# Turning three of four feed-forward tiles with VectorE blocks and partition copies instead of TensorE

## The chip, the cores and the metric

The kernel runs on one core of one Trainium2 chip. Everything is float32. The metric is the device time of one execution in microseconds, as the median of several runs. Shorter is better.

## The reference

Two blocks of a transformer run one after the other over 256 tokens of width 2048. The first block has two layers; each ends in the feed-forward part that the change touches:

```python
D_MODEL = 2048; SEQ = 256; D_FF = 4 * D_MODEL; DEPTH = 2

def squared_relu_mlp(h, w1, w2):
    z = jax.nn.relu(h @ w1)
    return (z * z) @ w2

for i in range(DEPTH):
    ...                                   # pooling or differential attention, memory attention
    x = x + jnp.concatenate([token_out, mem_out], axis=-1) @ w_out[i]
    x = x + squared_relu_mlp(rms_norm(x, ffn_norm[i]), w_ff1[i], w_ff2[i])
```

The second block (a linear recurrence, windowed attention, gates and projections) is not touched.

## The kernel before

**Weights.** All large products are cut into groups of 512 output columns over a contraction of 2048. A group has eight slabs (S = 8) of 256 rows by 512 columns of weight, 512 KB each. SP loads a slab into `raw` (line 740), ScalarE rounds it to `whi` (`hi`, line 876), VectorE computes the rest `wlo = raw - whi` (`lo`, line 1180), and TensorE multiplies: for each of two weight tiles and two token blocks, three matmuls of 512 columns (lines 1683 to 1685), 12 in a slab. There are four slots (RAW = 4): SP may refill a slot once VectorE has read it, and ScalarE may overwrite `whi` once TensorE has multiplied that slot's previous slab. So ScalarE and VectorE run at most some three slabs ahead of TensorE. Groups alternate between two accumulators `acc`.

**Order.** Each engine runs its own program, written slab by slab: first its work on the slab, then the steps that the schedule places behind it. Engines run in order; a step that waits holds everything behind it on that engine.

**Feed-forward.** The 8192 hidden columns are done in four chunks (NCHUNK = 4) of 2048. A chunk has four groups of the first product (w_ff1) and four of the second (w_ff2), 16 groups' worth of x-updates over the layer. Three chunks run as a hardware loop (`Fori`) of eight groups, k = 0 to 7, shifted by one: the loop's k = 0 to 2 are w_ff1 groups 1 to 3, k = 3 to 6 the w_ff2 groups, k = 7 the first w_ff1 group of the next chunk. The last chunk is written out. Behind slab 1 of k = 0 to 3 comes the end of the w_ff1 group that has just been finished: ScalarE takes it out of `acc` with a scale and a ReLU (`epi_relu2`, line 927), VectorE squares it into `stage_b` (line 1212), which holds 256 tokens as two blocks of 128 partitions by 512 columns.

**The tail.** The second product needs the hidden tile with its columns on partitions. Behind slab 3 of the same group, TensorE transposes `stage_b` into the PSUM bank `tp` with eight 128x128 transposes (`tail`, line 1701). Behind slab 5 ScalarE rounds `tp` into `set_hi` (line 992) and VectorE writes the rest into `set_lo` (line 1275). There are four tails in a chunk, 32 in the two layers. In k = 3, TensorE waits ahead of slab 0 for the first three tails and ahead of slab 6 for the fourth.

**x-updates.** Behind slab 1 of k = 4 to 7 VectorE adds a finished w_ff2 group to `x` (line 1650).

**Pool queue.** GpSimd only issues DMAs: `pool_w`, `mem_again` (memory tiles for the second layer), and spills and loads of the second block.

Of the kernel before, what the change touches and what calls it, by code (L numbers as in the profile page):

```python
# [10 lines left out]
TOK = 256  # L11
TB = TOK // P
D = 2048
NK = D // P
GW = 512
# [86 lines left out]
class Schedule:  # L102


    def __init__(self):
        self.groups = []
        self.woven = {}
        self.ends = {}
        self.lent = {}
        self.steps = {e: {} for e in ("pe", "act", "dve", "pool")}  # L110
        self.tails = 0
        self.staged = 0
        self.halves = 0
        self.info = {}
        self.norms = 0
        self.loops = {}
# [96 lines left out]
def plan():  # L213
# [64 lines left out]
    def ffn(layer, rst, a, z, next_rst, next_gain):  # L278

        first = sc.group(f"w_ff1{layer}", 0, 0, a)  # L280
        sc.groups[first].need[0] = [("tail_lo", sc.tails - 1)]
        sc.groups[first].need[S - 2] = [("tail_lo", sc.tails)]
        sc.loops[first + 1] = dict(layer=layer, tail0=sc.tails, staged0=sc.staged, rst=rst, a=a, z=z)
        for _ in range(8 * (NCHUNK - 1)):
            sc.group(None, 0, 0, a)
        sc.tails += 4 * (NCHUNK - 1)
        sc.staged += 4 * (NCHUNK - 1)
# [168 lines left out]
def build(nc, A, out):  # L456
# [6 lines left out]
    with ctx:  # L463
# [92 lines left out]
        def tail_bank(lent):  # L556

            if lent == "sd":
                return sd
            return tp if lent is None else acc[lent % 2]  # L560
# [6 lines left out]
        def pair_scales(i, hh):  # L567
# [12 lines left out]
        out_of = [sem("group_out0"), sem("group_out1")]  # L580
        names = ("tail_tp", "tail_hi", "tail_lo", "staged", "x_stat", "rstd_ok", "stage_th",
                 "att_in", "att_qk", "att_score", "att_smx", "att_exp", "att_prob", "att_pt", "att_ptc",
# [190 lines left out]
        def _(pool):  # L773
# [70 lines left out]
            def x_back(a):  # L844
# [4 lines left out]

            steps = dict(pool_w=pool_w, mem_again=mem_again, x_spill=x_spill, gate_store=gate_store,  # L850
                         gate_load=gate_load, merge_store=merge_store, merge_load=merge_load, lru_w=lru_w,
                         x_back=x_back)
            for s in sorted(sc.steps["pool"]):
                for name, args in sc.steps["pool"][s]:
                    steps[name](*args)


        @block.scalar
        def _(act):
# [122 lines left out]
            def tail(t, dst, kt, gain, lent=None):  # L982
                t = t if isinstance(t, N) else N(t)
                tp = tail_bank(lent)
                act.wait_ge(sm["tail_tp"], at(t + 1))
                if dst == "ut":
                    ins = A_(ut_tiles(kt, 2), tp[:, 0:2 * TOK].rearrange("p (n t) -> p n t", n=2), ACT.Copy)
                elif dst == "gt":
                    act.wait_ge(sm["x_out"], 16)
                    ins = A_(gt[:, TOK * kt:TOK * (kt + 2)], tp[:, 0:2 * TOK], ACT.Copy)  # L990
                elif gain is None:
                    ins = A_(sets[dst][0][:, TOK * kt:TOK * (kt + 4)], tp[:], ACT.Copy)  # L992
# [147 lines left out]
            for kind, g, info in segments():  # L1140
# [4 lines left out]
                else:  # L1145
                    with act.Fori(0, NCHUNK - 1) as c:
                        cc = N(0, 1, c)
                        for k in range(8):
                            for s in range(S):
                                hi(cc * 8 + (g + k), s)  # L1150
                                q = cc * 4 + (info["staged0"] + k)
                                t = cc * 4 + (info["tail0"] + k)
                                if s == 1 and k < 4:
# [7 lines left out]
        def _(dve):  # L1161
# [98 lines left out]
            def tail(t, dst, kt, gain, lent=None):  # L1260
# [11 lines left out]
                h, l = sets[dst]  # L1272
                if gain is None:
                    c = slice(TOK * kt, TOK * (kt + 4))
# [7 lines left out]
                ins.then_inc(sm["tail_lo"], 1)  # L1282


            def per_head(t, like, width):
# [315 lines left out]
            def epi_last(g, i):  # L1601
# [5 lines left out]
                for b in range(TB):  # L1607
# [6 lines left out]
                         epi_sigm=epi_sigm, epi_proj_a=epi_proj_a, epi_proj_b=epi_proj_b, x_rstd=x_rstd,  # L1614
                         tail=tail, norm_sum=norm_sum, norm_root=norm_root, norm_scale=norm_scale,
                         norm_rope=norm_rope, rope_gains=rope_gains,
# [13 lines left out]
            for kind, g, info in segments():  # L1630
# [4 lines left out]
                else:  # L1635
                    with dve.Fori(0, NCHUNK - 1) as c:
                        cc = N(0, 1, c)
                        for k in range(8):
                            for s in range(S):
                                lo(cc * 8 + (g + k), s)  # L1640
                                q = cc * 4 + (info["staged0"] + k)
                                t = cc * 4 + (info["tail0"] + k)
                                if s == 1 and k < 4:
                                    epi_relu2(cc * 8 + (g + k - 1), info["rst"], q, t)
                                if s == 5 and k < 4:
                                    tail(t, info["z"], 4 * k, None)
# [17 lines left out]
        def _(pe):  # L1664
# [215 lines left out]
            for kind, g, info in segments():  # L1880
# [7 lines left out]
                else:  # L1888
                    with pe.Fori(0, NCHUNK - 1) as c:
                        cc = N(0, 1, c)  # L1890
                        for k, (w, r, col, src) in enumerate(loop_groups(info, cc)):
                            for s in range(S):
                                if k == 3 and s in (0, S - 2):
                                    pe.wait_ge(sm["tail_lo"], at(cc * 4 + (info["tail0"] + (3 if s == 0 else 4))))
# [76 lines left out]
```

## Time and profile before

| | us |
|---|---|
| median of 3 runs | 3082.58 (3082.22 to 3083.31) |
| profiled execution, its own time | 3082.89 |
| its span in the trace | 3081.1 |
| TensorE matmul busy | 3024.2 |
| VectorE busy | 1760.4 |
| ScalarE busy | 1498.4 |
| GpSimd busy | 51.0 |

The granted TensorE clock is 0.997 of full speed over the span. The profiled execution is 1.8 us longer than its span and 0.3 us above the median of the runs. Times in the trace are microseconds from the span's start.

### The profile page before, as it was taken

Reading aid. Unit: us, or ns where it says so; the run is one execution under the profiler, and the core shown is the slowest. Engines: PE = TensorE matmul, PEld = TensorE weight load, DVE = VectorE, ACT = ScalarE, POOL = GpSimd, SP = SyncE. Lnnn points to the kernel's source line nnn. Section 1 sums busy time; section 2 is a strip of 40 time slices with the busy share of each in tenths; the row PEclk is TensorE's granted clock in tenths of the full one; section 3 lists DMA queues with packets and bytes.
Section 4 is the critical chain, followed back from the end, with each engine's and each line's share of the span. In section 5 each row is a group of like instructions: output and inputs, shape, how many; then the busy total and the mean of one; then the engine's idle time right before and its main releaser. Section 6 shows DMA issues by size and latency. Waiting matters only on the chain.

```text
span 3081.1 us, 37226 instructions
## 1 busy us (share of the span) xinstructions
PE 3024.2 (98%) x13900; PEld 2503.5 (81%) x13900; DVE 1760.4 (57%) x2334; ACT 1498.4 (49%) x2019; POOL 51.0 (2%) x81
## 2 busy tenths in 40 slices
PE   8999999999999999999999999999999999999998
PEld 6877888888888778778888888888888888787886
DVE  6536554545455676865554545455556557786554
ACT  6534434434344565654434444344444547786333
POOL 0000000000000000000000000000000000010000
PEclk9999999999999999999999999999999999999999
DMA  7545565565655555545565665655775555665664
GB/s 255 183 129 173 191 198 184 191 190 187 194 178 185 170 165 158 165 147 188 191 196 186 192 185 190 189 175 199 217 206 180 154 174 166 197 209 198 225 239 151
DMA packets 301161, 573.80 MB, mean 186 GB/s; under 512 B 18640, under 2 KB 43600, under 8 KB 300240
## 3 DMA queue, kind: packets, MB, share of 16 engines
q1 hardware_dynamic: 293248, 541.13, 55.8%
q0 software_dynamic: 7184, 29.63, 2.8%
q8 instruction: 103, 1.69, 0.2%
q10 hardware_dynamic: 576, 0.94, 0.1%
q14 instruction: 50, 0.41, 0.0%
HBM read 561.15 MB, written 10.49 MB: 186 GB/s over the span
## 4 chain that ended last, share of the span: by engine, by line
PE 85%; DVE 7%; ACT 5%; issue 2%; DMA 1%; DVEq 0%; ACTq 0%
PE acc L1683 26%; PE acc L1685 26%; PE acc L1684 26%; PE tp L1701 2%; DVE wlo L1180 2%; ACT whi L876 1%; DVE wlo L1175 1%; PE sd L1764 1%; PE sd L1746 1%; ACT prob L1093 1%; PE sd L1852 1%; ACT qk L1101 0%; ACT whi L879 0%; ACT L1093 0%; DVE set_lo L1279 0%
## 5 line engine op out<-in xcount | busy, mean ns | idle before, releaser
L1683 PE MATMUL acc<-whi,set_hi 128*128 128x512 f32 x4096 | 1620.2, 396 | 25.0 <-DVE wlo L1180 15.8
L1685 PE MATMUL acc<-whi,set_lo 128*128 128x512 f32 x4096 | 1597.3, 390 | 0.0
L1684 PE MATMUL acc<-wlo,set_hi 128*128 128x512 f32 x4096 | 1596.7, 390 | 0.0
L1180 DVE TENSOR_TENSOR wlo<-raw,whi 128x1024 fp32r<-128x1024 f32 x944 | 1130.4, 1222 | 592.6 <-ACT whi L876 591.7
L876 ACT ACTIVATE whi<-raw 128x1024 fp32r<-128x1024 f32 x944 | 969.9, 1057 | 642.1 <-PE acc L1685 611.7
L1683 PEld LDWEIGHTS acc<-whi,set_hi 128*128 128x128 f32 x4096 | 770.4, 188 | 197.7 <-DVE wlo L1180 25.8
L1685 PEld LDWEIGHTS acc<-whi,set_lo 128*128 128x128 f32 x4096 | 770.1, 188 | 162.8
L1684 PEld LDWEIGHTS acc<-wlo,set_hi 128*128 128x128 f32 x4096 | 770.8, 188 | 154.2
L1275 DVE TENSOR_TENSOR set_lo<-tp,set_hi 128x1024 fp32r<-128x1024 f32 x40 | 49.0, 1225 | 197.3 <-ACT set_hi L992 197.3
L992 ACT ACTIVATE set_hi<-tp 128x1024 fp32r<-128x1024 f32 x40 | 41.1, 1026 | 209.4 <-PE tp L1701 209.4
L1175 DVE SCALAR_TENSOR_TENSOR wlo<-raw,par,whi 128x512 fp32r<-128x512 f32 x160 | 111.9, 748 | 53.0 <-ACT whi L879 52.2
L1212 DVE TENSOR_TENSOR stage_b<-stage_a 128x1024 f32<-128x1024 f32 x32 | 39.2, 1225 | 142.2 <-ACT stage_a L927 142.2
L879 ACT ACTIVATE whi<-raw,par 128x512 fp32r<-128x512 f32 x160 | 103.8, 716 | 18.5 <-DMA raw<-in_w_kv 8.1
L927 ACT ACTIVATE stage_a<-acc,small 128x512 f32<-128x512 f32 x64 | 40.6, 686 | 140.3 <-PE acc L1685 140.3
L1279 DVE SCALAR_TENSOR_TENSOR set_lo<-tp,par,set_hi 128x256 fp32r<-128x256 f32 x96 | 39.8, 478 | 72.6 <-ACT set_hi L995 72.6
L995 ACT ACTIVATE set_hi<-tp,par 128x256 fp32r<-128x256 f32 x96 | 37.7, 478 | 71.8 <-PE tp L1701 71.8
L1650 DVE TENSOR_TENSOR x<-acc,x 128x1024 f32<-128x1024 f32 x24 | 29.4, 1225 | 74.9 <-PE acc L1685 74.9
L966 ACT ACTIVATE qk<-x 128x512 f32<-128x512 f32 x40 | 25.0, 632 | 90.5 <-DVE x L1207 90.5
L1701 PEld LDWEIGHTS tp<-const,stage_b 128*128 128x128 f32 x352 | 41.1, 140 | 5.8
L1701 PE MATMUL tp<-const,stage_b 128*128 128x128 f32 x352 | 45.6, 272 | 0.0
L1207 DVE TENSOR_TENSOR x<-acc,x 128x1024 f32<-128x1024 f32 x16 | 19.6, 1224 | 43.3 <-PE acc L1685 43.3
L1069 ACT ACTIVATE set_hi<-sd 128x512 fp32r<-128x512 f32 x12 | 7.2, 598 | 48.1 <-PE sd L1825 48.1
(229 smaller groups left out, 1167.0 us busy)
## 6 DMA issues: line engine op xcount, KB each, us to landing
raw<-in_w_ff SPq DMA_DIRECT2D x512, 512.0 KB, 4.5
raw<-in_w_in SPq DMA_DIRECT2D x248, 512.0 KB, 4.3
raw<-in_w_out SPq DMA_DIRECT2D x96, 512.0 KB, 4.4
raw<-in_w_mem_kv SPq DMA_DIRECT2D x32, 512.0 KB, 4.7
raw<-in_w_proj_a SPq DMA_DIRECT2D x32, 512.0 KB, 4.2
raw<-in_w_proj_b SPq DMA_DIRECT2D x32, 512.0 KB, 5.4
raw<-in_w_kv SPq DMA_DIRECT2D x48, 256.0 KB, 3.3
raw<-in_w_in SPq DMA_DIRECT2D x48, 256.0 KB, 3.7
```

Source lines behind the costliest of these rows:

```text
L876: A_(whi[:, c], raw[:, c], ACT.Copy).then_inc(w_hi, 1)
L879: ins = A_(whi[:, c], raw[:, c], ACT.Copy, scale=gain_of(fold, SLAB_K * s + t))
L927: ins = A_(stage_a[:, GW * b:GW * (b + 1)], a[:, GW * b:GW * (b + 1)], ACT.Relu, scale=rstd[k][:, b:b + 1])
L992: ins = A_(sets[dst][0][:, TOK * kt:TOK * (kt + 4)], tp[:], ACT.Copy)
L1175: ins = V.scalar_tensor_tensor(out=wlo[:, c], in0=raw[:, c], scalar=gain_of(fold, SLAB_K * s + t), in1=whi[:, c].bitcast(f32), op0=ALU.mul ...
L1180: V.tensor_tensor(wlo[:, c], raw[:, c], whi[:, c].bitcast(f32), ALU.subtract).then_inc(w_lo, 1)
L1275: ins = V.tensor_tensor(l[:, c], tp[:], h[:, c].bitcast(f32), ALU.subtract)
L1279: ins = V.scalar_tensor_tensor(out=l[:, c], in0=tp[:, TOK * j:TOK * (j + 1)], scalar=gain_of(gain, kt + j), in1=h[:, c].bitcast(f32), op0= ...
L1683: T.matmul(o, h[:, tok], whi[:, c], start=first, stop=False)
L1684: T.matmul(o, h[:, tok], wlo[:, c], start=False, stop=False)
L1685: ins = T.matmul(o, l[:, tok], whi[:, c], start=False, stop=last)
L1701: ins = T.transpose(tp[:, o:o + P], source_tile(src, j, b), ident)
```

## The change

Of the four tails of each chunk, the first three (24 of 32) no longer use TensorE. Instead:

- **turn** (VectorE, behind slab 1, straight after the square): two `transpose` instructions, one for each token block, 128 partitions by 512 columns, which turn each 32x32 block in place of the block and write `blocks`, the first half of the idle buffer `u`. It waits for the square's own semaphore.
- **shuffle** (Pool queue): waits for the turn and issues 16 DMAs, each of 32 partitions by 256 elements (32 KB) from partitions 32q of `blocks` to partitions 32d of `turned`, the second half of `u`. All count up one semaphore, 256 for a tile.
- **split**: ScalarE's rounding and VectorE's rest now stand behind slab 1 of the next group, ahead of that group's `epi_relu2`, and read `turned` in SBUF in place of `tp`. ScalarE waits for all 16 DMAs. On VectorE the order there is `lo` of slab 1, split of the last tile, square, turn, `lo` of slab 2.
- **waits of TensorE** in k = 3: two splits ahead of slab 0, the third ahead of slab 4, the fourth ahead of slab 6.
- The fourth tail of a chunk stays as it was.
- On the Pool queue all shuffles are written out, in order of slabs with its other steps; steps that stand behind a feed-forward part in the schedule (`mem_again` of the second layer) are now issued after its shuffles.

```diff
+    def turned(self, slab_turn, slab_split, source, dst, kt, gain=None):
+        t, n = self.tails, self.turns
+        self.tails += 1
+        self.turns += 1
+        self.at("dve", slab_turn, "turn", t, source)
+        self.at("pool", slab_turn, "shuffle", t, n)
+        self.at("act", slab_split, "tail", t, dst, kt, gain, ("turned", n))
+        self.at("dve", slab_split, "tail", t, dst, kt, gain, ("turned", n))
+        return t
...
-            sc.tail(S * (g + 1) + 3, S * (g + 1) + 5, ("staged", sc.staged), z, 4 * i)
+            if i < 3:
+                sc.turned(S * (g + 1) + 1, S * (g + 2) + 1, ("staged", sc.staged), z, 4 * i)
+            else:
+                sc.tail(S * (g + 1) + 3, S * (g + 1) + 5, ("staged", sc.staged), z, 4 * i)
...
-                sc.groups[g].need[0] = [("tail_lo", sc.tails - 1)]
-                sc.groups[g].need[S - 2] = [("tail_lo", sc.tails)]
+                for k, left in ((0, 2), (S - 4, 1), (S - 2, 0)):
+                    sc.groups[g].need[k] = [("tail_lo", sc.tails - left)]
...
+        blocks, turned = u[:, 0:TB * GW], u[:, TB * GW:2 * TB * GW]
...
+            def shuffle(t, n):
+                pool.wait_ge(sm["tail_tp"], at(t + 1))
+                for q in range(4):
+                    for d in range(4):
+                        dma(turned[32 * d:32 * (d + 1), 256 * q:256 * (q + 1)],
+                            blocks[32 * q:32 * (q + 1), 256 * d:256 * (d + 1)]).then_inc(sm["shuffled"], 16)
...
+            def turn(t, source):
+                source_ready(dve, source)
+                for b in range(TB):
+                    o = blocks.rearrange("p (d m b t) -> p b m d t", d=4, m=4, b=TB)[:, b]
+                    ins = V.transpose(o, stage_b[:, GW * b:GW * (b + 1)].rearrange("p (m d t) -> p m d t", m=4, d=4))
+                ins.then_inc(sm["tail_tp"], 1)
...
                     (VectorE's loop; ScalarE's is the same without the turn)
+                                if s == 1 and 1 <= k < 4:
+                                    tail(cc * 4 + (info["tail0"] + k - 1), info["z"], 4 * (k - 1), None, ("turned", None))
                                 if s == 1 and k < 4:
                                     epi_relu2(cc * 8 + (g + k - 1), info["rst"], q, t)
-                                if s == 5 and k < 4:
+                                if s == 1 and k < 3:
+                                    turn(t, ("staged", q))
+                                if s == 5 and k == 3:
                                     tail(t, info["z"], 4 * k, None)
...
-                                if s == 3 and k < 4:
+                                if s == 3 and k == 3:
                                     tail(cc * 4 + (info["tail0"] + k), ("staged", cc * 4 + (info["staged0"] + k)))
```

## Rows read from the trace of the kernel before

**Rows 1.** The page's first lines and its busy times by engine

```profile
span 3081.1 us, 37226 instructions
...
PE 3024.2 (98%) x13900; PEld 2503.5 (81%) x13900; DVE 1760.4 (57%) x2334; ACT 1498.4 (49%) x2019; POOL 51.0 (2%) x81
```

**Rows 2.** The page's chain that ended last, by engine

```profile
PE 85%; DVE 7%; ACT 5%; issue 2%; DMA 1%; DVEq 0%; ACTq 0%
```

**Rows 3.** Windows view, first layer's feed-forward: width, busy times (count), clock, DMA

```profile
318.00:990.00 672.00, 672.00 (x3038) 557.89 (x3038) 342.86 (x290) 285.08 (x302) 0.00 (x0) 1.00 0.59 188
```

**Rows 4.** Timeline of ScalarE, the ends of two w_ff1 groups: start, us

```profile
537.01 1.27 ACT L927 ACTIVATE stage_a<-acc,small 128x512 f32<-128x512 f32 x2 [4.38 <-PE acc L1685]
...
559.67 1.27 ACT L927 ACTIVATE stage_a<-acc,small 128x512 f32<-128x512 f32 x2 [4.38 <-PE acc L1685]
560.82 2.95 ACT L876 ACTIVATE whi<-raw 128x1024 fp32r<-128x1024 f32 x3
...
571.43 1.03 ACT L992 ACTIVATE set_hi<-tp 128x1024 fp32r<-128x1024 f32 x1 [5.26 <-PE tp L1701]
```

**Rows 5.** Timeline of VectorE in the same stretch and behind it

```profile
560.97 1.23 DVE L1212 TENSOR_TENSOR stage_b<-stage_a 128x1024 f32<-128x1024 f32 x1 [4.42 <-ACT stage_a L927]
562.11 3.49 DVE L1180 TENSOR_TENSOR wlo<-raw,whi 128x1024 fp32r<-128x1024 f32 x3
...
572.49 1.22 DVE L1275 TENSOR_TENSOR set_lo<-tp,set_hi 128x1024 fp32r<-128x1024 f32 x1 [5.06 <-ACT set_hi L992]
...
582.35 1.23 DVE L1650 TENSOR_TENSOR x<-acc,x 128x1024 f32<-128x1024 f32 x1 [3.12 <-PE acc L1685]
...
604.11 1.23 DVE L1650 TENSOR_TENSOR x<-acc,x 128x1024 f32<-128x1024 f32 x1 [3.12 <-PE acc L1685]
```

**Rows 6.** The chain in order of time, one tail: start, us

```profile
570.52 0.87 PE tp L1701 x8
```

**Rows 7.** Timeline of TensorE, first matmuls of slab 0 and slab 2

```profile
559.47 0.39 PE L1683 MATMUL acc<-whi,set_hi 128*128 128x512 f32 x1
...
564.91 0.39 PE L1683 MATMUL acc<-whi,set_hi 128*128 128x512 f32 x1
```

**Rows 8.** Timeline where TensorE waited for a late weight slab

```profile
1432.30 3.49 DVE L1180 TENSOR_TENSOR wlo<-raw,whi 128x1024 fp32r<-128x1024 f32 x3
...
1432.87 0.39 PE L1685 MATMUL acc<-whi,set_lo 128*128 128x512 f32 x1
...
1433.58 0.50 PE L1683 MATMUL acc<-whi,set_hi 128*128 128x512 f32 x1 [0.32 <-DVE wlo L1180]
...
1433.91 0.39 PE L1684 MATMUL acc<-wlo,set_hi 128*128 128x512 f32 x1
```

**Rows 9.** Timeline of VectorE, two 512-column instructions in a row

```profile
3003.48 1.29 DVE L1608 TENSOR_TENSOR kv<-acc,u 128x512 f32<-128x512 f32 x2 [4.42 <-ACT qk L949]
3004.69 3.49 DVE L1180 TENSOR_TENSOR wlo<-raw,whi 128x1024 fp32r<-128x1024 f32 x3
```

**Rows 10.** Groups of VectorE by shape: busy us, mean ns

```profile
L1175 DVE SCALAR_TENSOR_TENSOR wlo<-raw,par,whi 128x512 fp32r<-128x512 f32 x160 | 111.9, 748 | 53.0 <-ACT whi L879 52.2
```

**Rows 11.** Timeline of the Pool queue, DMAs issued in a row

```profile
187.10 1.42 POOL L801 DMA_DIRECT2D mkv<-in_mem  x2
...
2498.79 0.71 POOL L818 DMA_DIRECT2D kv<-gate_spill  x1 [27.52 <-DVE ob L1465]
...
2501.61 0.71 POOL L841 DMA_DIRECT2D kv<-in_lru_w_i  x1
```

**Rows 12.** Lines 841 and 832: issue ns and landing us (min/median/max)

```profile
L841 POOL DMA_DIRECT2D kv<-in_lru_w_i x16: 709/710/723, 2500.2 to 2764.6; - x16
...
DMA to landing us min/median/max: 2.9/4.3/6.7
...
L832 POOL DMA_DIRECT2D mkv<-merge_spill x4: 531/531/536, 2814.3 to 2938.0; - x4
```

**Rows 13.** DMA issues by line: count, KB each, median us to landing

```profile
raw<-in_w_ff SPq DMA_DIRECT2D x512, 512.0 KB, 4.5
```

More of the change, by code:

```diff
@@ L1 @@
+import itertools
 import math
@@ L282, in ffn @@
         sc.groups[first].need[S - 2] = [("tail_lo", sc.tails)]
-        sc.loops[first + 1] = dict(layer=layer, tail0=sc.tails, staged0=sc.staged, rst=rst, a=a, z=z)
+        sc.loops[first + 1] = dict(layer=layer, tail0=sc.tails, staged0=sc.staged, turn0=sc.turns, rst=rst, a=a, z=z)
         for _ in range(8 * (NCHUNK - 1)):
@@ L556, in tail_bank @@
         def tail_bank(lent):
+            if isinstance(lent, tuple):
+                return turned.rearrange("p (q n t) -> p n q t", q=4, t=32)
             if lent == "sd":
@@ L848, in x_back @@
                 dma(gpost, A["post"]).then_inc(sm["post_in"], 16)
-            steps = dict(pool_w=pool_w, mem_again=mem_again, x_spill=x_spill, gate_store=gate_store,
+            def shuffle(t, n):
[4 more added lines that the diff above has]
+                            blocks[32 * q:32 * (q + 1), 256 * d:256 * (d + 1)]).then_inc(sm["shuffled"], 16)
+            steps = dict(shuffle=shuffle, pool_w=pool_w, mem_again=mem_again, x_spill=x_spill, gate_store=gate_store,
                          gate_load=gate_load, merge_store=merge_store, merge_load=merge_load, lru_w=lru_w,
                          x_back=x_back)
-            for s in sorted(sc.steps["pool"]):
-                for name, args in sc.steps["pool"][s]:
-                    steps[name](*args)
+            slabs = sorted(sc.steps["pool"])
+            for g, info in list(sc.loops.items()) + [(GALL + 1, None)]:
+                while slabs and slabs[0] < S * g:
+                    for name, args in sc.steps["pool"][slabs.pop(0)]:
+                        steps[name](*args)
+                if info:
+                    for c, k in itertools.product(range(NCHUNK - 1), range(3)):
+                        shuffle(4 * c + info["tail0"] + k, 3 * c + info["turn0"] + k)
         @block.scalar
@@ L984, in tail @@
                 tp = tail_bank(lent)
-                act.wait_ge(sm["tail_tp"], at(t + 1))
+                if isinstance(lent, tuple):
+                    act.wait_ge(sm["shuffled"], at((lent[1] + 1) * 256))
+                else:
+                    act.wait_ge(sm["tail_tp"], at(t + 1))
                 if dst == "ut":
@@ L990, in tail @@
                     ins = A_(gt[:, TOK * kt:TOK * (kt + 2)], tp[:, 0:2 * TOK], ACT.Copy)
+                elif isinstance(lent, tuple):
+                    o = sets[dst][0][:, TOK * kt:TOK * (kt + 4)]
+                    ins = A_(o.rearrange("p (n q t) -> p n q t", q=4, t=32), tp, ACT.Copy)
                 elif gain is None:
@@ L1152, in _ @@
                                 t = cc * 4 + (info["tail0"] + k)
+                                if s == 1 and 1 <= k < 4:
+                                    n = cc * 3 + (info["turn0"] + k - 1)
+                                    tail(cc * 4 + (info["tail0"] + k - 1), info["z"], 4 * (k - 1), None, ("turned", n))
                                 if s == 1 and k < 4:
                                     epi_relu2(cc * 8 + (g + k - 1), info["rst"], q, t)
-                                if s == 5 and k < 4:
+                                if s == 5 and k == 3:
                                     tail(t, info["z"], 4 * k, None)
@@ L1272, in tail @@
                 h, l = sets[dst]
-                if gain is None:
+                if isinstance(lent, tuple):
+                    c = slice(TOK * kt, TOK * (kt + 4))
+                    o, i = (w[:, c].rearrange("p (n q t) -> p n q t", q=4, t=32) for w in (l, h))
+                    ins = V.tensor_tensor(o, tp, i.bitcast(f32), ALU.subtract)
+                elif gain is None:
                     c = slice(TOK * kt, TOK * (kt + 4))
@@ L1614, in _ @@
                          epi_sigm=epi_sigm, epi_proj_a=epi_proj_a, epi_proj_b=epi_proj_b, x_rstd=x_rstd,
-                         tail=tail, norm_sum=norm_sum, norm_root=norm_root, norm_scale=norm_scale,
+                         tail=tail, turn=turn, norm_sum=norm_sum, norm_root=norm_root, norm_scale=norm_scale,
                          norm_rope=norm_rope, rope_gains=rope_gains,
@@ L1642, in _ @@
                                 t = cc * 4 + (info["tail0"] + k)
+                                if s == 1 and 1 <= k < 4:
+                                    tail(cc * 4 + (info["tail0"] + k - 1), info["z"], 4 * (k - 1), None, ("turned", None))
                                 if s == 1 and k < 4:
                                     epi_relu2(cc * 8 + (g + k - 1), info["rst"], q, t)
-                                if s == 5 and k < 4:
+                                if s == 1 and k < 3:
+                                    turn(t, ("staged", q))
+                                if s == 5 and k == 3:
                                     tail(t, info["z"], 4 * k, None)
@@ L1892, in _ @@
                             for s in range(S):
-                                if k == 3 and s in (0, S - 2):
-                                    pe.wait_ge(sm["tail_lo"], at(cc * 4 + (info["tail0"] + (3 if s == 0 else 4))))
+                                if k == 3 and s in (0, S - 4, S - 2):
+                                    ready = info["tail0"] + {0: 2, S - 4: 3, S - 2: 4}[s]
+                                    pe.wait_ge(sm["tail_lo"], at(cc * 4 + ready))
                                 of = cc * 8 + (g + k)
                                 slab(of, s, of, s, src, s == 0, s == S - 1)
-                                if s == 3 and k < 4:
+                                if s == 3 and k == 3:
                                     tail(cc * 4 + (info["tail0"] + k), ("staged", cc * 4 + (info["staged0"] + k)))
```

4 lines of the change are left out of this document (3 added, 1 removed).

## The prediction

> **What bounds the kernel now.** I read the page's busy times first. TensorE's matmuls cover 98% of the span, VectorE 57%, and GpSimd 2% [rows 1]; the chain that ended last is TensorE for 85% [rows 2]. A busy share can hide waits, so I asked the windows view for the stretch that the change is about. In the first layer's feed-forward TensorE is busy for 672.00 of 672.00 us at granted clock 1.00 [rows 3]: it never waits there, and a group costs what its instructions cost. Work taken from TensorE is then worth its whole price, as long as nothing else comes to hold it.
>
> What a tail costs TensorE comes from the periods. The ends of two neighbouring w_ff1 groups, with a tail between them, stand 559.67 - 537.01 = 22.66 us apart [rows 4]; two neighbouring w_ff2 groups, the same 96 matmuls without a tail, 604.11 - 582.35 = 21.76 us [rows 5]. A tail costs 0.90 us. The chain shows the same thing directly, 0.87 us for eight transposes [rows 6]; the rest is a slightly slower restart.
>
> The second thing to see is how far the helpers are ahead at the end of a group, since that is where the change puts its work. I set the clock to 0 at the start of the ReLU (559.67). TensorE has slabs 0 and 1 ready, and its slab 0 has just begun (559.47); it comes to slab 2 at 564.91, that is +5.24 [rows 7]. VectorE squares at +1.30 and starts `lo` of slab 2 at 562.11, +2.44 [rows 5]. What a late `lo` costs I read where one was late [rows 8]: it started at 1432.30, TensorE went on at 1433.58, 1.28 later; it was due at 1432.87 + 0.23 = 1433.10; and the next matmul came 0.33 in place of 0.23 behind the first, another 0.10. So the loss is start of `lo` + 1.38 - due. Here that is 2.44 + 1.38 - 5.24 = -1.42: there are 1.42 us of cover for new work on VectorE at this place, and no more.
>
> **Part 1, what is removed.** 24 tails of 0.90 us on the path that sets the end: -21.6 us. The eight remaining tails cost what they did.
>
> **Part 2, the turn.** It stands between the square and `lo` of slab 2, thus exactly in the 1.42 us. First it waits for the square's own result. Before, `lo` started 1.14 behind the square although that takes 1.23 [rows 5], as unrelated instructions overlap a little; with the wait it is some 1.26, so +0.12. Then come two transposes of 128x512. The trace has no VectorE transpose. From below: two 512-column instructions in a row took 1.21 until the next began [rows 9], 0.60 each, and I know no reason for less. From above among ordinary instructions: 748 ns each without overlap [rows 10]. I take 0.69, the length of one of rows 9 without any overlap ((1.29 - 0.60) = 0.69), because an instruction of another kind that strides in 32-element runs will hardly do better: 1.38. Loss for a tile: 0.12 + 1.38 - 1.42 = 0.08, which I round to 0.10 as the matmuls behind a stop run a little wide. Ends: 0.12 + 1.21 - 1.42 < 0, no loss; 0.12 + 1.50 - 1.42 = 0.20. For 24 tiles: 2.4 us, with ends 0 and 4.8. `lo` of slabs 3 and 4 need no more: VectorE does one in 1.13 (3.49 for three less overlap) and TensorE takes 21.76/8 = 2.72 a slab.
>
> On this cost a rule can be weighed. The Trainium skill (VectorE: DVE Perf Modes, The three transpose paths) gives 311 ns for a 128x128 transpose in bf16, in 32x32 blocks; 384 further columns at one a cycle of 0.96 GHz would make an estimate of 0.71 us for ours, if four-byte elements go at the same rate. By it the loss is 0.12 + 1.42 - 1.42 = 0.12 a tile and the time 3064. No run here has shown it yet.
>
> **Part 3, the split moves a group later.** ScalarE's 1.03 us (571.43) and VectorE's 1.22 (572.49) are taken out of the place behind slab 5 and put ahead of the ReLU of the next group. There ScalarE stands idle 4.38 us [rows 4] and VectorE 4.42 us [rows 5] before the group ends, both waiting for TensorE. So they cost nothing, if the DMAs are there. The bank `tp` or the SBUF buffer as input I take as equal: the SBUF-to-SBUF rounding takes under 1.06 (2.95 for three). TensorE's wait for the third tile ahead of slab 4 of k = 3 lies at +5.24 + 5.44 = +10.7, its split is done by +1.3. If this cover is gone (DMAs late), the delay passes one for one to ReLU, square, turn and `lo` of slab 2, as all stand behind the split on their engines.
>
> **Part 4, the shuffle.** The turn ends at +1.30 + 1.26 + 1.38 = +3.94. The next ReLU is due at +21.76. Without loss ScalarE must have finished its 1.06 by then: the last DMA must have landed by +20.7. VectorE is a little freer (20.7 + 1.06 + 1.23 = 22.99 against 21.76 + 1.30 = 23.06). The budget is 20.7 - 3.94 = 16.8 us. The trace has no DMA from SBUF to SBUF. The Pool queue issued five in a row at 0.71 each [rows 11]; an issue took 0.53 for plain rows and 0.71 for the two-part ones, landing 2.9 to 6.7 after the issue began, median 4.3 [rows 12]. Ours have 32 rows of 1 KB, fewer than any of these, so I take 0.53: 15 x 0.53 + 4.3 = 12.3 us, 4.5 to spare. From below, 15 x 0.53 + 2.9 = 10.9; from above, 15 x 0.71 + 6.7 = 17.4, which is 0.6 late, or 14 us over 24 tiles. I cost it at 0 and keep 14 for the range.
>
> The Pool queue has nothing else to issue in a feed-forward part (x0 in rows 3). `mem_again`, issued at 187.10 before [rows 11], now waits behind the first layer's shuffles; its data are wanted three slabs into the first group after the part, over four groups (87 us) behind the last shuffle: no cost. The weight loads: `lo` of slab 2 ends 1.5 later, so SP issues slab 6 at about +5.2, it lands 4.5 later [rows 13] at +9.7, ScalarE and VectorE need 2.3, and TensorE comes to it at +5.24 + 4 x 2.72 = +16.1. 4.1 us are spare, and the shuffles add 0.5 MB a group to the 4 MB of weights, on DMA engines that are busy 0.59 of the time [rows 3].
>
> **Sum.** 3082.9 (the profiled execution) - 21.6 + 2.4 = 3063.7; the median of the runs is 0.3 lower: 3063.4. Its own range: 3061 (no loss) to 3066 (0.20 a tile), with a few us for a shuffle that is at times late: 3060 to 3071.
>
> **Rivals.**
> - *The 32x32 turn runs at half rate.* Four-byte blocks may go through in two passes. Each instruction then lasts as a 1024-column one, 1.22 [rows 5]: loss 0.12 + 2.44 - 1.42 = 1.14 a tile, against 0.90 saved: +5.8, 3088. With overlap (1.14 each) 3085. The point at which it decides: 1.10 us a transpose makes the change worth nothing. For it: no row shows the operation. Against it: the plain four-byte operations in the rows all go at one rate, 0.69 for 512 columns and 1.22 for 1024 [rows 5, 9].
> - *The shuffle is late* (this one ends on the slow side). Place: ScalarE's wait for 16 landings. From an issue of (16.8 - 4.3)/15 = 0.83 us on, each further us of lateness is a us on every one of 24 tiles; at 0.8 late the saving is gone, an issue of 0.89. At 1.0 an issue: 2.5 late, loss 2.6, +1.7 a tile, +41: 3123. For it: sixteen in a row is three times as many as any row shows, and they compete with weight traffic. Against: five in a row kept 0.71 while VectorE and SP were at work [rows 11, 12].
> - *Half hidden.* Both of the last at small size, say a turn of 0.85 each and a shuffle late now and then by 0.3: loss 0.7, 24 x 0.2 = 4.8 saved, 3078 (range 3071 to 3082).
> - *No effect*, since TensorE was held by something else: rows 3 speak against it, and I count it into the last.
>
> A rule speaks for the second. The Trainium skill (DMA: Bandwidth & Descriptors, Anatomy of one DMA) puts the fixed cost of a Pool-queue DMA at about 2.0 us, and calls transfers below 64 KB mostly overhead. If the 16 paid it one after the other, that would be an estimate of 32 us, 15 past the budget. The five issues at 0.71 with landings of some 4.3 show that they overlap.
>
> **Chances.** Forecast 0.66; half rate 0.10; late shuffle beyond break-even 0.13; half hidden 0.11. Faster by over 0.2% (6.2 us, about what a measurement of this kernel can tell from no change) are the forecast and half of half-hidden: 0.71. Within 0.2%: the other half and half of half-rate, 0.11. Slower: 0.18. The range 3060 to 3089 holds the forecast, half-hidden and half rate, 0.87; I keep the upper end because both unknown prices reach there (the Pool rows' worst landing with the slow turn, 0.20 + 0.6 = 0.8 a tile, gives 3080).
>
> **What would show it.** Right: w_ff1 groups with a turned tile 21.8 to 21.9 us apart; two transposes of about 0.69; `lo` of slab 2 starting 3.9 behind the ReLU; TensorE's idle time on `wlo` at slab 2 under 0.15 each; ScalarE's split starting some 17 us behind the previous ReLU, ahead of its idle wait for TensorE; 16 Pool issues in 8.5 us. Wrong: ScalarE waiting for a DMA in the feed-forward, VectorE transposes over 1 us, TensorE stopped over 0.5 us at slab 2, or weight slabs that ScalarE waits for.

## The result and the profile after

The changed kernel took 3059.7 us (median of 4 runs, 3059.61 to 3060.36) against 3082.4 for the kernel before: ratio 0.9926, 95% interval 0.9914 to 0.9939, 22.7 us faster. The profiled execution took 3060.36 with a span of 3058.6, where that of before had 3082.89 and 3081.1. The forecast was 3063.4 with a range from 3060.0: the mechanism came as told, the change gained more than was reckoned, and the time lies 0.3 us below the range.

The page of the changed kernel: span, busy times, and the new groups (busy us, mean ns, idle before and who ended it).

```profile
span 3058.6 us, 37252 instructions
...
PE 3002.9 (98%) x13708; PEld 2484.1 (81%) x13708; DVE 1793.7 (59%) x2382; ACT 1504.9 (49%) x2019; POOL 239.2 (8%) x465
...
L875 POOL DMA_DIRECT2D u<-u x384 | 188.2, 498 | 1509.2 <-DVE u L1336 1474.1
...
L1318 DVE TENSOR_TENSOR set_lo<-u,set_hi 128x1024 fp32r<-128x1024 f32 x24 | 29.3, 1219 | 5.4 <-ACT set_hi L1029 5.4
L1336 DVE STREAM_TRANSPOSE u<-stage_b 128x512 f32<-128x512 f32 x48 | 31.3, 691 | 0.8
```

TensorE does 192 instructions less (24 tails of eight) and is 21.3 us less busy; VectorE gained 33.3 us, the Pool queue 188.2 us for 384 DMA issues of 498 ns. Next to none of that is on the path, as the experiments show.

The timelines of the stretch that answers to [rows 4, 5]: ScalarE, then VectorE, then the Pool queue.

```profile
531.94 1.27 ACT L960 ACTIVATE stage_a<-acc,small 128x512 f32<-128x512 f32 x2 [3.43 <-PE acc L1743]
...
541.53 1.06 ACT L909 ACTIVATE whi<-raw 128x1024 fp32r<-128x1024 f32 x1 [3.09 <-DMA raw<-in_w_ff]
...
549.66 1.05 ACT L1029 ACTIVATE set_hi<-u 128x1024 fp32r<-128x1024 f32 x1
553.72 1.27 ACT L960 ACTIVATE stage_a<-acc,small 128x512 f32<-128x512 f32 x2 [3.01 <-PE acc L1743]
```

```profile
533.24 1.23 DVE L1254 TENSOR_TENSOR stage_b<-stage_a 128x1024 f32<-128x1024 f32 x1 [3.29 <-ACT stage_a L960]
534.50 1.31 DVE L1336 STREAM_TRANSPOSE u<-stage_b 128x512 f32<-128x512 f32 x2
535.73 4.59 DVE L1222 TENSOR_TENSOR wlo<-raw,whi 128x1024 fp32r<-128x1024 f32 x4
```

```profile
536.10 7.84 POOL L875 DMA_DIRECT2D u<-u  x16 [13.94 <-DVE u L1336]
```

What to see: the two ReLUs stand 553.72 - 531.94 = 21.78 us apart, where it was 22.66 [rows 4] and 21.76 is the period without a tail [rows 5]. The turn begins 1.26 behind the square, as reckoned, and the next weights 1.23 behind the turn's start. The split runs at 549.66, and ScalarE still has 3.01 us to wait for TensorE ahead of the next ReLU. The last of 16 DMAs is issued at about 543.4. The turned groups hold no wait of TensorE: it is busy for all of 591.3 us from the first to the last ReLU of the first layer.

Two signs that the prediction had listed under wrong did appear, and cost nothing. ScalarE waits for raw weights (541.53), 66 times in the two feed-forward parts, where it did once before. And the split waits for the shuffle at three of the 24 tiles, 5.9 us in all. At two of these, the third tile of the hardware loop's last chunk in each layer, the Pool queue began its issues some 3.1 us later than at its neighbours, for nothing that the trace names; both traces of the changed kernel have it at the same two tiles. The Pool queue, then ScalarE:

```profile
689.36 7.83 POOL L875 DMA_DIRECT2D u<-u  x16 [13.87 <-DVE u L1336]
714.25 7.83 POOL L875 DMA_DIRECT2D u<-u  x16 [17.06 <-issue]
```

```profile
727.48 1.06 ACT L1029 ACTIVATE set_hi<-u 128x1024 fp32r<-128x1024 f32 x1 [3.08 <-DMA u<-u]
728.77 1.27 ACT L960 ACTIVATE stage_a<-acc,small 128x512 f32<-128x512 f32 x2 [0.24 <-PE acc L1743]
```

The ReLU before stood at 706.99, so this split starts at +20.5 where +20.7 was reckoned as the last moment: 0.2 us to spare in place of the 4.5 of the prediction.

### The profile page after: what moved, and what is told of

Read it like the earlier page. It is cut to its first block, busy times and chain, and to the rows that moved or that the text cites. A ratio compares the mean times of both kernels' runs of the same rounds, so it can differ in the third digit from the quotient of the medians.

```text
span 3058.6 us, 37252 instructions
## 1 busy us (share of the span) xinstructions
PE 3002.9 (98%) x13708; PEld 2484.1 (81%) x13708; DVE 1793.7 (59%) x2382; ACT 1504.9 (49%) x2019; POOL 239.2 (8%) x465
## 3 DMA queue, kind: packets, MB, share of 16 engines
q8 instruction: 84, 1.38, 0.2%
## 4 chain that ended last, share of the span: by engine, by line
PE 84%; DVE 8%; ACT 6%; issue 2%; DMA 0%; ACTq 0%; DVEq 0%
PE acc L1741 26%; PE acc L1743 26%; PE acc L1742 26%; ACT whi L909 2%; DVE wlo L1222 2%; PE tp L1759 1%; DVE wlo L1217 1%; ACT prob L1132 1%; PE sd L1822 1%; PE sd L1804 1%; PE sd L1910 1%; ACT qk L1140 0%; ACT whi L912 0%; ACT L1132 0%; PE sd L1900 0%
## 5 line engine op out<-in xcount | busy, mean ns | idle before, releaser
L1741 PE MATMUL acc<-whi,set_hi 128*128 128x512 f32 x4096 | 1618.6, 395 | 24.4 <-DVE wlo L1222 15.5
L875 POOL DMA_DIRECT2D u<-u x384 | 188.2, 498 | 1509.2 <-DVE u L1336 1474.1
L1321 DVE TENSOR_TENSOR set_lo<-tp,set_hi 128x1024 fp32r<-128x1024 f32 x16 | 19.6, 1225 | 76.6 <-ACT set_hi L1031 76.6
L1031 ACT ACTIVATE set_hi<-tp 128x1024 fp32r<-128x1024 f32 x16 | 16.4, 1026 | 83.9 <-PE tp L1759 83.9
L1318 DVE TENSOR_TENSOR set_lo<-u,set_hi 128x1024 fp32r<-128x1024 f32 x24 | 29.3, 1219 | 5.4 <-ACT set_hi L1029 5.4
L1336 DVE STREAM_TRANSPOSE u<-stage_b 128x512 f32<-128x512 f32 x48 | 31.3, 691 | 0.8
```

Of the source, the lines that this page charges most:

```text
L875: dma(turned[32 * d:32 * (d + 1), 256 * q:256 * (q + 1)], blocks[32 * q:32 * (q + 1), 256 * d:256 * (d + 1)]).then_inc(sm["shuffled"], 16)
L1741: T.matmul(o, h[:, tok], whi[:, c], start=first, stop=False)
```

## The experiments

Each ratio below is against the kernel before on the same chip. The kernel before, run again as an experiment, gave 1.0002 (0.9993 to 1.0011), which shows how little the comparison can tell apart: about 3 us. To see smaller amounts I use the traces: the time from the first to the last ReLU of each feed-forward part, which holds 12 of the 24 turned tiles. Its other groups take the same in both kernels: from a chunk's last ReLU to the next chunk's first it is 109.7 to 109.8 us.

**The kernel before again (3082.03 us).** No edit.

> The kernel before, unchanged, profiled and timed again. In its first trace the groups that the change doesn't touch were 0.57 us longer at one place near 40 to 66 us and 0.55 us at 1804 us than in the trace of the changed kernel. Theory A (those are chance, they come and go between executions): at least one of the two is gone from this trace, and the span is 0.5 to 1 us shorter than the first. Theory B (they belong to the kernel before): both stand at the same place. Median 3081.9 to 3082.9 either way.

**The changed kernel again (3058.96 us, ratio 0.9922, 0.9909 to 0.9936).** No edit.

> The changed kernel, unchanged, timed again. Theory A: the span differs from the first by up to 1 us, while each group that holds a turned tile is again 21.78 us (0.88 less than 22.66); the medians differ by 24 x 0.88 = 21.1 plus at most 1.5. Theory B: medians differ by 22.5 or more in every round.

One line each of the view by line of the ReLU (min/median/max ns, first and last start), in the first and then the second feed-forward part; first the kernel before in its first trace, then in its second, then the changed kernel in its first and its second.

```profile
L927 ACT ACTIVATE stage_a<-acc,small x32: 682/686/690, 314.0 to 915.8; 128x512 f32<-128x512 f32 x32
L927 ACT ACTIVATE stage_a<-acc,small x32: 682/685/690, 1448.4 to 2050.9; 128x512 f32<-128x512 f32 x32
```

```profile
L927 ACT ACTIVATE stage_a<-acc,small x32: 682/686/690, 313.5 to 915.4; 128x512 f32<-128x512 f32 x32
L927 ACT ACTIVATE stage_a<-acc,small x32: 681/685/691, 1444.7 to 2047.8; 128x512 f32<-128x512 f32 x32
```

```profile
L960 ACT ACTIVATE stage_a<-acc,small x32: 682/686/692, 313.3 to 904.6; 128x512 f32<-128x512 f32 x32
L960 ACT ACTIVATE stage_a<-acc,small x32: 682/686/690, 1437.1 to 2028.3; 128x512 f32<-128x512 f32 x32
```

```profile
L960 ACT ACTIVATE stage_a<-acc,small x32: 682/686/690, 312.7 to 904.0; 128x512 f32<-128x512 f32 x32
L960 ACT ACTIVATE stage_a<-acc,small x32: 682/686/690, 1436.4 to 2027.7; 128x512 f32<-128x512 f32 x32
```

The first part took 601.8 and 601.9 before, 591.3 and 591.3 after: 10.5 us for 12 tiles, 0.88 each. The second took 602.5 and 603.1 before, 591.2 and 591.3 after. There the kernel before loses 0.7 to 1.2 us more, and one row of its second trace, at the end of the hardware loop, shows where:

```profile
1801.02 0.49 PE L1683 MATMUL acc<-whi,set_hi 128*128 128x512 f32 x1 [0.92 <-issue]
```

TensorE stands there for nothing that the trace names. The two ReLUs around it are 23.23 us apart in the first trace and 23.91 in the second, where the others are at 22.65 to 22.69: a loss of 0.6 and 1.2 us. So neither of my two theories holds as written. The stop at the loop's end belongs to the kernel before (both of its traces have it, none of the changed kernel and its variants does). The one near 53 us is a wait for late weights that varies: 1.12 and 0.73 us before, 0.77 and 0.26 after.

The stretch between the two parts varies more: 532.6 us in the first trace of the kernel before, 529.3 in the second, with the same code. There the granted clock decides. In the first trace two slices of 10 us had 0.83, in the second none. Here is the later one of the first trace, and the same place in the second:

```profile
1320.00:1330.00 10.00, 7.79 (x38) 5.85 (x37) 6.97 (x16) 4.04 (x6) 0.00 (x0) 0.83 0.46 141
```

```profile
1320.00:1330.00 10.00, 7.79 (x44) 6.09 (x43) 7.31 (x14) 6.42 (x14) 0.00 (x0) 1.00 0.41 108
```

TensorE was busy for the same 7.79 us and did 38 matmuls in place of 44. Within the slice the clock fell to 0.50, the lower level of 1.2 GHz, after TensorE had stood 2.2 us for ScalarE; in the second trace the clock stayed at 1.00 there. Both traces of the changed kernel have two such slices (532.5 and 532.4 us), those of the kernels with hardly any turn and with the turn behind slab 2, both below, have one (530.8 and 530.8). So a slice costs about 1.6 us and comes and goes, and medians that differ by 2 us say nothing of the change.

**Almost no turn and no shuffle (3057.15 us, 0.9918, 0.9904 to 0.9932).**

```diff
-                for b in range(TB):
-                    o = blocks.rearrange("p (d m b t) -> p b m d t", d=4, m=4, b=TB)[:, b]
-                    ins = V.transpose(o, stage_b[:, GW * b:GW * (b + 1)].rearrange("p (m d t) -> p m d t", m=4, d=4))
-                ins.then_inc(sm["tail_tp"], 1)
+                V.transpose(blocks[:, 0:32], stage_b[:, 0:32]).then_inc(sm["tail_tp"], 1)
...
-                for q in range(4):
-                    for d in range(4):
+                for q in range(1):
+                    for d in range(1):
...
-                    act.wait_ge(sm["shuffled"], at((lent[1] + 1) * 256))
+                    act.wait_ge(sm["shuffled"], at((lent[1] + 1) * 16))
```

> Leaves out most of the turn and 15 of 16 transfers: the turn is one transpose of 128x32 and the shuffle one transfer, so the hidden tiles are wrong; the removed TensorE transposes stay removed. My theory (turn and shuffle are wholly hidden): 3059.7, within 0.5 us of the changed kernel, groups of 21.76. Rival (they cost TensorE something, by late weights or traffic): 1 to 5 us faster than the changed kernel.

The two ReLU lines of this kernel:

```profile
L960 ACT ACTIVATE stage_a<-acc,small x32: 682/686/690, 312.9 to 903.8; 128x512 f32<-128x512 f32 x32
L960 ACT ACTIVATE stage_a<-acc,small x32: 682/686/690, 1434.6 to 2025.5; 128x512 f32<-128x512 f32 x32
```

590.9 in both: turn and shuffle cost 0.3 to 0.4 us in 12 tiles, 0.7 in all. They are hidden but for 0.03 us a tile. The median is 1.8 below the changed kernel's second timing, more than the 0.5 expected. Of the 2.1 between their traces (spans of 3057.9 and 3055.8), 1.6 lies between the two parts, one slice at the lower clock less: that the rival's 1 to 5 us were hit is mostly chance.

**The turn twice (3085.79 us, 1.0012, 1.0002 to 1.0021).**

```diff
-                for b in range(TB):
-                    o = blocks.rearrange("p (d m b t) -> p b m d t", d=4, m=4, b=TB)[:, b]
+                for t, b in itertools.product((u[:, 2048:3072], blocks), range(TB)):
+                    o = t.rearrange("p (d m b t) -> p b m d t", d=4, m=4, b=TB)[:, b]
```

> The changed kernel with the two transposes done twice (the first time into an unused part of u), all else the same. If the cover behind the square is the 1.42 us of the prediction, of which wait and turn use 1.35, a second turn of 1.23 us is uncovered but for 0.07: 24 x 1.16 = 28 us, 3087 to 3090, TensorE stopping at slab 2 of each such group. Rival (VectorE is busy 59% and has room): within 2 us of 3059.7.

VectorE and then TensorE in one such group:

```profile
537.81 1.23 DVE L1254 TENSOR_TENSOR stage_b<-stage_a 128x1024 f32<-128x1024 f32 x1 [2.94 <-ACT stage_a L960]
539.07 2.49 DVE L1336 STREAM_TRANSPOSE u<-stage_b 128x512 f32<-128x512 f32 x4
541.48 4.59 DVE L1222 TENSOR_TENSOR wlo<-raw,whi 128x1024 fp32r<-128x1024 f32 x4
```

```profile
542.72 0.50 PE L1741 MATMUL acc<-whi,set_hi 128*128 128x512 f32 x1 [0.81 <-DVE wlo L1222]
543.06 0.39 PE L1742 MATMUL acc<-wlo,set_hi 128*128 128x512 f32 x1
```

`lo` of slab 2 starts 3.67 behind the square, which is +4.97 from the ReLU; the formula gives 4.97 + 1.38 - 5.24 = 1.11 a tile. Measured against the changed kernel: 3085.8 - 3059.0 = 26.8, 1.12 a tile. VectorE was idle 41% of the time, and the 1.2 us of the second turn still cost nearly all of themselves. The cover of 1.42 us is real, and the single turn uses it up.

**The turn twice, behind slab 2 (3057.89 us, 0.9923, 0.9909 to 0.9936).**

```diff
-                                if s == 1 and k < 3:
+                                if s == 2 and k < 3:
                                     turn(t, ("staged", q))
```

on top of the doubled turn, with the same step in the written-out chunk.

> The same doubled transposes, but behind slab 2 in place of slab 1, so that the weights of slab 2 go first. If the place is what counted in the doubled turn (22.9 us a group, 27 us in all), the cost goes: the four transposes of 0.62 end at about +6.1, the weights of slab 3 start there, 6.1 + 1.38 - 7.96 is below zero, and the DMAs still land by +18.7 of +20.7. Expected 3059, within 1 us of the changed kernel. Rival (VectorE's total load is the cost): 3080 or more.

Same work, 28 us less: the place was the cost. Its VectorE timeline shows the order, weights of slab 2 first:

```profile
533.06 1.22 DVE L1222 TENSOR_TENSOR wlo<-raw,whi 128x1024 fp32r<-128x1024 f32 x1
534.20 2.48 DVE L1336 STREAM_TRANSPOSE u<-stage_b 128x512 f32<-128x512 f32 x4
536.61 4.59 DVE L1222 TENSOR_TENSOR wlo<-raw,whi 128x1024 fp32r<-128x1024 f32 x4
```

**The single turn behind slab 2 (3057.53 us, 0.9920, 0.9905 to 0.9934).** The same edit on the changed kernel.

> The changed kernel with the (single) turn behind slab 2 in place of slab 1. In its trace the groups with a turn took 21.78 to 21.80 where 21.76 is the period without one. If that 0.02 to 0.04 is the turn just touching slab 2's weights, these groups become 21.76 and 24 x 0.025 = 0.6 us go, which runs can't tell from 0; the spans of the two feed-forward loops in the trace can. The DMAs start 1.2 later and still land by +17.5 of +20.7.

```profile
L960 ACT ACTIVATE stage_a<-acc,small x32: 682/686/690, 312.9 to 903.8; 128x512 f32<-128x512 f32 x32
L960 ACT ACTIVATE stage_a<-acc,small x32: 671/683/690, 1434.6 to 2025.6; 128x512 f32<-128x512 f32 x32
```

590.9 and 591.0, as the kernel with hardly any turn: the remaining 0.03 a tile is gone. ScalarE's waits for weights of w_ff1 and w_ff2 fell too, from 120.1 us in 66 waits to 42.2 in 22. It would fit that the third slab is freed earlier and SP refills it earlier, but no run tries that alone; with hardly any turn and shuffle it is 7.5 us in 4 waits.

The price is at the other end. The split now waits for the shuffle at 20 of the 24 tiles, 17.5 us in all, longest where the Pool queue begins late:

```profile
727.02 1.06 ACT L1029 ACTIVATE set_hi<-u 128x1024 fp32r<-128x1024 f32 x1 [3.20 <-DMA u<-u]
728.20 1.27 ACT L960 ACTIVATE stage_a<-acc,small 128x512 f32<-128x512 f32 x2
```

That split starts 20.58 behind the ReLU at 706.44, and the next ReLU is still on time, 21.76 behind it, with no wait for TensorE left: this is the budget's edge.

**Twice the transfers (3139.94 us, 1.0193, 1.0178 to 1.0209).**

```diff
-                for q in range(4):
+                for t, q in itertools.product((u[:, 3072:4096], turned), range(4)):
                     for d in range(4):
-                        dma(turned[32 * d:32 * (d + 1), 256 * q:256 * (q + 1)],
+                        dma(t[32 * d:32 * (d + 1), 256 * q:256 * (q + 1)],
...
-                    act.wait_ge(sm["shuffled"], at((lent[1] + 1) * 256))
+                    act.wait_ge(sm["shuffled"], at((lent[1] + 1) * 512))
```

> The changed kernel with 32 transfers a tile in place of 16: the first 16 are copies into an unused part of u, the ones that count come last. Budget theory: 31 x 0.50 + 4.9 = 20.4 us behind the turn's end at +3.8 is +24.2, 3.5 late. The two groups of a chunk with split, ReLU and turn lose 3.4 each, the one without a turn behind it about 2: 8 x 8.8 = 70 us, 3115 to 3145; ScalarE waits for the DMA in the split, TensorE at slab 2. Rival (the shuffle has no deadline that matters, or transfers overlap so well that twice as many land in time): under 3065.

The Pool queue and ScalarE in one group, and ScalarE's waits (total, times, longest):

```profile
366.46 15.66 POOL L875 DMA_DIRECT2D u<-u  x32 [8.70 <-DVE u L1336]
```

```profile
386.47 1.06 ACT L1029 ACTIVATE set_hi<-u 128x1024 fp32r<-128x1024 f32 x1 [6.16 <-DMA u<-u]
387.43 1.25 ACT L960 ACTIVATE stage_a<-acc,small 128x512 f32<-128x512 f32 x2
```

```profile
ACT set_hi L1029 <- DMA u<-u: 152.9, 24, 8.7
```

The split starts 386.47 - 366.46 = 20.0 behind the first issue, 20.4 expected, and all 24 splits wait. 81.0 us more than the second timing of the changed kernel, 3.4 a tile, against the budget's 3.5 late. So the deadline is where it was reckoned. How the loss falls on the three tiles of a chunk I had wrong: each of the three ReLU periods grew by 1.9 to 5.3 us, and the stretch behind them gave 1.4 back.

The mean granted clock was 0.99 here against 0.997, and for the same 13,708 matmuls TensorE was busy 3030.1 us in place of 3002.9. That is no second cause of the periods: all 24 ReLUs behind a split start as in the rows above, straight behind it and with no wait for TensorE, so the DMAs set when they start. It shows where nothing is late: the stretch of four w_ff2 groups and one w_ff1 group that holds a slice at 0.83 (760 to 770) took 110.02 us, the others without one 108.3 to 108.4.

**The fourth tile as well, half of its DMAs from ScalarE (3078.71 us, 0.9992, 0.9983 to 1.0001).**

```diff
+            def shuffle_act(t):
+                act.wait_ge(sm["tail_tp"], at(t + 1))
+                for q in (2, 3):
+                    for d in range(4):
+                        act.dma_start(turned[32 * d:32 * (d + 1), 256 * q:256 * (q + 1)],
+                                      blocks[32 * q:32 * (q + 1), 256 * d:256 * (d + 1)]).then_inc(sm["shuffled_act"], 16)
...
+                                if s == 4 and k == 3:
+                                    shuffle_act(t)
-                                if s == 5 and k == 3:
-                                    tail(t, info["z"], 4 * k, None)
+                                if s == 5 and k == 3:
+                                    tail(t, info["z"], 4 * k, None, ("turned", (cc + info["turn0"] // 4, k)))
```

Pool issues the other eight; TensorE's last tail goes.

> All four tiles of a chunk turned; no transposes of TensorE are left in the feed-forward. The fourth tile's 16 transfers are issued half by Pool and half by ScalarE (behind slab 4), its split stays behind slab 5. Expected: Pool's eight land at about 3.8 + 7 x 0.50 + 4.9 = +12.2, ScalarE's at about the same time, the split is done by +14.6, TensorE needs it at +16.1; eight tails of 0.88 go: 7 us faster than the changed kernel, 3052. Rival (eight transfers on ScalarE's queue hold up the weights of slab 5, or the split comes too late): TensorE stops in the first w_ff2 group, 3055 to 3070.

```profile
558.16 5.20 ACTq L1020 DMA_DIRECT2D u<-u  x8
563.48 1.06 ACT L909 ACTIVATE whi<-raw 128x1024 fp32r<-128x1024 f32 x1 [5.10 <-issue]
569.79 1.06 ACT L1040 ACTIVATE set_hi<-u 128x1024 fp32r<-128x1024 f32 x1 [5.25 <-DMA u<-u]
```

A miss: the rival's time was passed too. ScalarE stood 5.20 us for eight issues, 0.65 each, and the last, issued at 562.66, landed 7.1 later. The split came 569.79 - 554.27 = 15.5 behind the ReLU; the transfers were expected at +12.2 and the split done by +14.6. VectorE stands in order too: its weights for slab 6 waited for that split, and TensorE stopped 2.0 to 3.3 us at `wlo` in each of the eight chunks. The clock took its part: for the same 13,644 matmuls TensorE was busy 3002.8 us here and 2994.7 in the next kernel, which has no such stops; at three of the eight stops the granted clock fell (0.80 to 0.85 in the slices 390 to 400, 920 to 940 and 1880 to 1890).

**The fourth tile, with two slabs crossed (3052.25 us, 0.9903, 0.9887 to 0.9919).** All 16 DMAs from Pool; SP and TensorE take the first two slabs of the second w_ff2 group ahead of the last two of the first, the only ones that read the fourth tile.

```diff
+def crossed(k, s):
+    if (k, s) in ((0, 6), (0, 7)):
+        k, s = 1, s - 6
+    elif (k, s) in ((1, 0), (1, 1)):
+        k, s = 0, s + 6
+    return k, s, s == 0, s == NSLAB - 1
...
-                                if s == 1 and 1 <= k < 4:
+                                if (1 <= k < 4 and s == 1) or (k == 4 and s == 0):
...
-                                if s == 1 and k >= 4:
+                                if k >= 4 and s == (3 if k == 4 else 1):
...
-                                of = cc * 8 + (g + k)
-                                slab(of, s, of, s, src, s == 0, s == S - 1)
-                                if s == 3 and k == 3:
-                                    tail(cc * 4 + (info["tail0"] + k), ("staged", cc * 4 + (info["staged0"] + k)))
+                                at_ = cc * 8 + (g + k)
+                                if k in (3, 4):
+                                    j, ks, begins, ends = crossed(k - 3, s)
+                                    slab(at_, s, cc * 8 + (g + 3 + j), ks, src, begins, ends)
+                                else:
+                                    slab(at_, s, at_, s, src, s == 0, s == S - 1)
```

> All four tiles of a chunk turned, all 16 transfers by Pool as for the others, and time made for the fourth: TensorE and SP take slabs 6 and 7 of the first w_ff2 group, the only ones that read the fourth tile, behind slabs 0 and 1 of the second (whose accumulator is free by then). The fourth tile is then wanted at +5.24 + 6 x 2.72 = +21.6 in place of +16.1; the last DMA lands at 3.8 + 15 x 0.50 + 4.9 = +16.2, the split is over by about +18.5. The x-update of the first group moves behind slab 3. Expected: eight more tails of 0.88 gone, 7 us faster than the changed kernel, 3052 (3050 to 3054). Rival (something new stops TensorE there: the moved x-update, the split in that place, the weights): 3056 or more.

```profile
554.00 1.27 ACT L975 ACTIVATE stage_a<-acc,small 128x512 f32<-128x512 f32 x2 [2.19 <-PE acc L1756]
...
571.12 1.06 ACT L1044 ACTIVATE set_hi<-u 128x1024 fp32r<-128x1024 f32 x1 [2.24 <-DMA u<-u]
```

```profile
L975 ACT ACTIVATE stage_a<-acc,small x32: 682/686/690, 314.5 to 903.0; 128x512 f32<-128x512 f32 x32
L975 ACT ACTIVATE stage_a<-acc,small x32: 682/686/690, 1433.0 to 2021.5; 128x512 f32<-128x512 f32 x32
```

The split of the fourth tile starts at 571.12 - 554.00 = +17.1 and is through VectorE by +19.4, later than the +18.5 expected but ahead of +21.6. The parts take 588.5, 2.8 less than the changed kernel's, for the three fourth tiles between the first and the last ReLU; three tails of 0.90 are 2.7. 3052.25 is 6.7 below the second timing of the changed kernel and 29.5 below the kernel before: the fastest version here.

## Why the prediction was nearly right, and what it got wrong

**What bounds the kernel.** Right. The period of 21.78 with no wait of TensorE in the loops says that what is taken from TensorE is gained.

**Part 1, -21.6.** Right in mechanism and size. With next to no turn and shuffle, or with the turn behind slab 2, the part takes 590.9 us in place of 601.8: 10.9 for 12 tails, 0.91 each, 21.8 in all.

**Part 2, the turn, +2.4.** This term was mis-sized, by 1.7 us. I took 0.69 for each transpose without overlap. Its length was 691 ns, as taken, but two of them and the step to the weights took 1.23 in place of 1.38: they overlap as the pair in [rows 9] does. `lo` of slab 2 started at 535.73 - 531.94 = +3.79, and the formula gives 3.79 + 1.38 - 5.24 = -0.07, no loss. Measured: 0.03 a tile, 0.7 us. The lower end that I had written down for this term, 1.21, was close to the truth; I chose the upper value for a layout of 32-element runs, which cost no more than 0.02 beyond it. Formula and cover were right, as the doubled turn shows (1.12 a tile against 1.11 from its rows).

**Parts 3 and 4.** Right in what they cost, which is nothing, but with less to spare than was written. The split lay in the idle time; 16 issues took 7.84 us at 0.498 each, and the landing median was 4.9 against the 4.3 taken. From the turn's end that is 0.3 until the first issue + 15 x 0.50 + 4.9 = 12.7 (12.3 forecast). The budget's edge lies where it was reckoned: a split at +20.58 was on time, and the doubled shuffle's at +24.1 was not. What the prediction left out is that the Pool queue can begin late: 3.1 us at two of the 24 tiles, which left 0.2 us at one of them. The weight loads have become late for ScalarE 66 times, which I hadn't foreseen; I had reckoned 4.1 us of slack for TensorE, and it held.

**Sum and range.** The forecast's net was 21.6 - 2.4 = 19.2 us. Measured it is 21.1: 10.5 us in each part, 0.88 a tile, with the turn's 0.7 already in it. The profiled execution would then take 3082.9 - 21.1 = 3061.8. It took 3060.36. Of the 1.4 between, 0.6 is the stop at the loop's end, which the changed kernel hasn't, and 0.6 lies ahead of the first ReLU (313.95 against 313.31), where the kernel before happened to wait longer for data and weights. Last, the median came 0.7 below the profiled execution and not 0.3.

So two steps failed. The turn's term was 1.7 too high. With tails and turn as measured the forecast would have been 3061.5, inside the range, and still 1.8 above the result. And the sum took all else as fixed, with the one profiled execution as its base: a stop that belongs to the kernel before, waits at the start and slices at the lower clock were put at nothing (of the slices, both profiled executions happened to have two between the parts), and the range's lower end of 3060.0 left 1.0 us below a sum without any loss. Executions of one and the same kernel before spread from 3078.8 to 3084.1 later on, which the three runs shown (3082.2 to 3083.3) understate. That the result fell outside by 0.3, and not inside, is within this scatter.

**Rivals.** The turn at half rate fell at once (691 ns). The late shuffle needed twice the transfers to cost anything, though at two tiles it came near. Half hidden and no effect fell with the time: 0.88 of each tail's 0.90 was gained. The fixed 2.0 us of a Pool DMA (the Trainium skill, DMA: Bandwidth & Descriptors, Anatomy of one DMA) doesn't add up over DMAs issued in a row: 16 were issued in 7.84 us. The prediction's estimate of 0.71 us, worked out from the bf16 figure of the Trainium skill (VectorE: DVE Perf Modes, The three transpose paths), agrees with the 0.69 measured for four-byte elements.

**Left open.** What TensorE stands for at the end of the second hardware loop of the kernel before (0.92 us in one trace, "issue"), and why the changed programs don't. What the Pool queue stands for at two tiles. Why the clock falls behind a stop in one execution and not in another.

## What to carry to other kernels

When one engine never waits, price a step by the difference of two periods, with and without it, and then look for its new place by the time until the next instruction that the bound engine needs, not by how busy the helper is: 1.2 us more on a VectorE that idles 41% cost 27 us behind slab 1 and nothing behind slab 2. Many small transfers are fine if the deadline is a group away: what counts is issues times issue time plus one landing, and a few us to spare for a queue that begins late. Where a tile comes too late for its first reader, let the reader do something else first; crossing two slabs gave what issuing the DMAs from two queues did not.

## What the runs showed of the hardware that I had not expected

- VectorE's transpose of 128x512 float32 in 32x32 blocks takes 691 ns, and two in a row with the step to the next instruction 1.23 us, nearly the 1.21 of two plain 512-column instructions [rows 9].
- A DMA of 32 partitions by 1 KB costs the Pool queue 498 ns to issue, ScalarE's queue 0.61 us (median of 64), in which ScalarE does nothing else. Landing: 1.7 to 6.1 us after the issue from Pool, median 4.9; 1.8 to 7.5 from ScalarE, median 5.4.
- Executions of the same kernel differ by 3 us in a stretch of 530 us between the two feed-forward parts: slices of 10 us at a granted clock of 0.83, about 1.6 us each, two in one trace and none in the other.
